# One encoder layer: the first modulation weights in two halves by columns, weights waited for by piece, turned logits copied in front of y

## The reference, cut to what matters

```python
mod = (silu(c) @ w_ada + b_ada).reshape(B, 6, D)   # shift1, scale1, gate1, shift2, scale2, gate2
h = rmsnorm(x, g_pre_mix) * (1 + scale1) + shift1
x = x + gate1 * rmsnorm(token_mixer(h), g_post_mix)    # h @ w_in, mLSTM heads | attention heads, @ w_out
h = rmsnorm(x, g_pre_ffn) * (1 + scale2) + shift2
aff = softmax(h @ w_router)                            # 16 experts, each takes its top 128 tokens
x = x + gate2 * rmsnorm(experts(h, aff), g_post_ffn)
```

## Time and profile before

| | |
|---|---|
| median of 3 runs | 2425.46 us (2424.74 to 2425.91) |
| profiled execution | 2422.2 us, span 2420.4 us |
| TensorE busy | 2286.9 us, 94% |
| DVE, ScalarE, GpSimd busy | 1206.9 us (50%), 1103.8 us (46%), 605.3 us (25%) |
| mean granted TensorE clock | 0.98 |
| start until the first product of h @ w_in | 37.8 us, TensorE busy 14.28 us of it |
| GpSimd, root of the mean squares (L792) | 1.05 us for the first quarter, 1.93 us for the second |
| GpSimd, split of half unit 1 of w_in (L803) | 2.54 us for two pieces, from 41.70 |
| DVE, normalising a quarter (L1371) | 2.74 us for four |

### The profile page before, as it was taken

How to read it: one execution, slowest core, us unless ns; L and a number is a source line. 1 busy time by engine, 2 the same in 40 slices (tenths; PEclk the granted TensorE clock), 3 DMA queues, 4 the chain that set the end, 5 groups by cost and what they waited for, 6 DMA issues and landing times. The chain is left out here.

```text
span 2420.4 us, 34918 instructions
## 1 busy us (share of the span) xinstructions
PE 2286.9 (94%) x13449; PEld 1905.4 (79%) x13449; DVE 1206.9 (50%) x1879; ACT 1103.8 (46%) x1826; POOL 605.3 (25%) x675
## 2 busy tenths in 40 slices
PE   6999999999999998999936999999999999999996
PEld 3679989777999896677725888888888888888885
DVE  3222334654323446665565555544445556666664
ACT  4223444655434436665532444444444454545552
POOL 3004332433143424430021011111010122222433
PEclk9999999999999999999967999999999999999998
DMA  8845445657464558764455566666666678888775
GB/s 311 250 119 185 144 159 190 196 149 178 115 201 136 191 163 233 217 184 155 170 212 220 195 224 210 224 215 216 204 204 232 212 277 305 321 313 291 278 290 165
DMA packets 239038, 511.46 MB, mean 211 GB/s; under 512 B 36981, under 2 KB 128005, under 8 KB 235825
## 3 DMA queue, kind: packets, MB, share of 16 engines
q1 hardware_dynamic: 190960, 394.78, 48.5%
q0 software_dynamic: 47936, 114.77, 16.1%
HBM read 415.32 MB, written 93.69 MB: 210 GB/s over the span
## 5 line engine op out<-in xcount | busy, mean ns | idle before, releaser
L2465 DVE TENSOR_TENSOR moe_w_lo<-moe_wf,moe_w_hi 128x2048 fp32r<-128x2048 f32 x192 | 439.6, 2292 | 457.0 <-ACT moe_w_hi L2343 457.0
L2343 ACT ACTIVATE moe_w_hi<-moe_wf 128x2048 fp32r<-128x2048 f32 x192 | 368.0, 1917 | 549.4 <-PE moe_acc L2575 549.3
L2575 PE MATMUL moe_acc<-moe_w_hi,moe_x_hi 128*128 128x512 f32 x1024 | 403.0, 394 | 1.7 <-DVE moe_x_lo L2471 1.4
L2575 PE MATMUL moe_acc<-moe_w_hi,moe_x_lo 128*128 128x512 f32 x1024 | 399.9, 391 | 0.0
L2575 PE MATMUL moe_acc<-moe_w_lo,moe_x_hi 128*128 128x512 f32 x1024 | 399.6, 390 | 0.0
L2575 PEld LDWEIGHTS moe_acc<-moe_w_hi,moe_x_hi 128*128 128x128 f32 x1024 | 193.0, 188 | 41.9 <-DVE moe_x_lo L2471 1.8
L2575 PEld LDWEIGHTS moe_acc<-moe_w_hi,moe_x_lo 128*128 128x128 f32 x1024 | 192.9, 188 | 40.6
L2575 PEld LDWEIGHTS moe_acc<-moe_w_lo,moe_x_hi 128*128 128x128 f32 x1024 | 193.1, 189 | 39.1
L1785 PE MATMUL banks<-fr_w_hi,fr_h_hi 128*128 128x256 f32 x768 | 223.2, 291 | 0.0
L1785 PE MATMUL banks<-fr_w_lo,fr_h_hi 128*128 128x256 f32 x768 | 217.0, 283 | 0.0
L1785 PE MATMUL banks<-fr_w_hi,fr_h_lo 128*128 128x256 f32 x768 | 217.0, 283 | 0.0
(11 more groups left out here) (282 smaller groups left out, 4055.8 us busy)
## 6 DMA issues: line engine op xcount, KB each, us to landing
moe_wf<-in_w_expert_gate SPq DMA_DIRECT2D x64, 1024.0 KB, 4.9
moe_wf<-in_w_expert_up SPq DMA_DIRECT2D x64, 1024.0 KB, 5.0
moe_wf<-in_w_expert_down SPq DMA_DIRECT2D x64, 1024.0 KB, 7.1
fr_w_raw<-in_w_units SPq DMA_DIRECT2D x28, 1024.0 KB, 6.6
fr_bias<-in_na_bias SPq DMA_DIRECT2D x16, 1520.0 KB, 11.4
fr_a_w<-in_w_ada POOLq DMA_DIRECT2D x16, 1024.0 KB, 8.8
scratch_qk_t<-fr_stage SPq DMA_DIRECT2D x64, 256.0 KB, 2.6
scratch_vov<-fr_stage SPq DMA_DIRECT2D x96, 128.0 KB, 2.2
```

What stands on the lines that cost most here:

```text
L2343: nc.scalar.activation(w_hi[:, q, :, :], wf[:, q, :, :], ACT.Copy).then_inc(w_hi_ready, 1)
L2465: nc.vector.tensor_tensor(w_lo[:, q, :, :], wf[:, q, :, :], w_hi[:, q, :, :].bitcast(F32), ALU.subtract).then_inc(w_lo_ready, 1)
L2575: mm = nc.tensor.matmul(acc[:, j, b, :], x[:, g, k, :], w[:, q, a, h * HALF:(h + 1) * HALF], start=(k == 0 and i == 0), stop=(k == KC - 1 ...
```

## The change

Three things. First, the first round of w_ada comes in sixteen pieces of 0.5 MB: for each k the columns 0 to 511 and 1024 to 1535 (the first half of shift1 and of scale1, rows of 2 KB), then half unit 0 of w_in, then the other columns. The first half of the modulation is multiplied, copied, turned and added alone, and k 0 to 3 of h and of blocks 0 and 1 are done on it; the second half's products stand between these four ticks, and the last two turns of x too. Second, a block waits for the first piece of its weights only, and for the second in the tick that uses it. Third, in the output stage `take_parts` stands in front of `take_y`. Some semaphores are shared to make room.

```diff
@@ SP
-                sp.dma_start(a_w[:, k, :], ada_view[k, :, 0:4 * HALF]).then_inc(a_first[k // 2], 16)
+                sp.dma_start(ada_part(a_w[:, k, :], 0), ada_part(ada_view[k, :, 0:4 * HALF], 0)).then_inc(a_first[k // 2], 16)
             load_w(0)
+            for k in range(KC):
+                sp.dma_start(ada_part(a_w[:, k, :], 1), ada_part(ada_view[k, :, 0:4 * HALF], 1)).then_inc(a_o_loaded[k], 16)
             load_x(1)
             load_w(1)
@@ ScalarE, output stage
+                    if 2 <= t <= N_TILES + 1 and t != N_TILES:
+                        take_parts(t - 2)
                     if t < N_TILES:
                         take_y(t, 0)
                         need(act, omean_ready, 2 * t - 1)
                         out_squares(h2[:, t % 2, :], 0, (0,))
-                    if 2 <= t <= N_TILES + 1 and t != N_TILES:
-                        take_parts(t - 2)
@@ ScalarE, start
-            for k in range(KC):
-                take_x(k)
-            act.drain()
-            a_row_first()
-            split_w(0, 0)
-            for k in range(KC):
-                make_h(0, k)
-                if k == 1:
-                    split_w(0, 1)
-                if k >= 4:
-                    squares(1, k - 4)
+            a_row_first(0)
+            for half in range(2):
+                for k in range(4 * half, 4 * half + 4):
+                    take_x(k)
+                act.drain()
+                split_w(0, half)
+                if half:
+                    a_row_first(1)
+                for k in range(4 * half, 4 * half + 4):
+                    make_h(0, k)
+            for j in range(4):
+                squares(1, j)
@@ DVE
+            def modulation(half):
+                dve.wait_ge(mod_turned, 2 + half)
+                ks = slice(4 * half, 4 * half + 4)
+                for which in range(2):
+                    turned_mods = ps[:, MOD_BANKS[half][which], 0:4 * GROUPS].rearrange("p (k g) -> p k g", g=GROUPS)
+                    bias_ = b_cols[:, which * KC + 4 * half:which * KC + 4 * half + 4]
+                    nc.vector.tensor_tensor(mods[:, which, ks, :], turned_mods, bias_.unsqueeze(2).to_broadcast([P, 4, GROUPS]), ALU.add)
+                dve.drain()
+                for g in range(GROUPS):
+                    a = nc.vector.scalar_tensor_tensor(scale[:, g, ks], mods[:, 1, ks, g], 1.0, g_pre[:, ks], ALU.add, ALU.mult)
+                a.then_inc(scale_ready, 1)
...
+            for half in range(2):
+                a_row_first(half)
+                modulation(half)
+                if half == 0:
+                    split_w(0, 0)
+                for k in range(4 * half, 4 * half + 4):
+                    split_h(0, k)
+                if half == 0:
                     split_w(0, 1)
-            mean_of(1)
             for piece in range(2):
                 split_w(1, piece)
+            mean_of(1)
@@ TensorE
+            def ada_first(k, half):
+                if half:
+                    pe.wait_ge(a_o_loaded[k], 16)
+                else:
+                    pe.wait_ge(a_first[k // 2], 32)
+                for j in (half, 2 + half):
+                    mm = nc.tensor.matmul(ps[32 * j:32 * j + 2, (PO, PA)[half], :], c_silu[:, k, :], a_w[:, k, j * HALF:(j + 1) * HALF],
+                                          start=(k == 0), stop=(k == KC - 1))
+                mm.then_inc((a_early, a_done)[half], 1)
...
-                        pe.wait_ge(w_lo_ready, 2 * hu + 2)
+                        pe.wait_ge(w_lo_ready, 2 * hu + 1)
                     need(pe, evac_done, b - 1)
                     for u in range(TICKS):
+                        if hu != GATE_UNIT and u == (1 if form(b)[2] == "t" else 2):
+                            pe.wait_ge(w_lo_ready, 2 * hu + 2)
...
             for k in range(KC):
-                ada(0, k)
+                ada_first(k, 0)
                 if k == 1:
                     pe.wait_ge(cols_loaded, 48)
                     nc.tensor.transpose(ps[:, PS, 0:2 * KC], b_rows[:, :], ident[0:2 * KC, 0:2 * KC]).then_inc(mod_turned, 1)
-                if 2 <= k < 6:
-                    turn_x(0, 2 * k - 4)
-                    turn_x(0, 2 * k - 3)
...
+            for k in range(6):
+                turn_x(0, k)
+                if k == 1:
+                    turn_mods(0)
+            for k in range(4):
+                fill.tick(1)
+                if k in (1, 2):
+                    turn_x(0, 5 + k)
+                ada_first(2 * k, 1)
+                ada_first(2 * k + 1, 1)
+            turn_mods(1)
```

More of the change, by code:

```diff
@@ L426, in front @@
         PX = 7
+        PA, MOD_BANKS = 3, ((2, 4), (5, 4))
+        first_bank = lambda k: k % 2 if k < 4 else 6 + k % 2
         A_ROUNDS = 3
@@ L1039, in take_x, with a_row_first @@
                 act.wait_ge(turned, k + 1)
[L1040 to L1045, removed]
+                nc.scalar.activation(h_raw[:, k, 0:HALF], ps[:, first_bank(k), :], ACT.Copy).then_inc(xT_ready, 1)
+            def a_row_first(half):
+                act.wait_ge((a_early, a_done)[half], KC)
+                at_ = slice(32 * half, 32 * half + 2)
+                nc.scalar.activation(a_row[at_, 0, :], ps[at_, (PO, PA)[half], :], ACT.Copy).then_inc(a_row_ready, 1)
             def make_h(q, k):
@@ L1079, in split_o @@
                 c, a = i // 4, i % 4
[L1080 removed]
+                act.wait_ge(a_o_loaded[i], 32)
                 cut = (slice(None), slice(2 * a, 2 * a + 2), slice(c * HALF, (c + 1) * HALF))
@@ L1183, in stream @@
                         if t == N_TILES:
-                            act.wait_ge(x1_half, 1)
+                            act.wait_ge(row_half, 1)
                             out_squares(ox[:, (t - 1) % 2, :], 1, (0,))
@@ L1379, in split_h, with a_row_first @@
                 nc.vector.tensor_tensor(h_lo[:, k, cut], h_raw[:, k, cut], h_hi[:, k, cut].bitcast(F32), ALU.subtract).then_inc(h_ready, 1)
[L1381 to L1384, removed]
+            def a_row_first(half):
+                dve.wait_ge((a_early, a_done)[half], KC)
+                at_ = slice(64 + 32 * half, 66 + 32 * half)
+                nc.vector.tensor_copy(a_row[at_, 0, :], ps[at_, (PO, PA)[half], :]).then_inc(a_row_ready, 1)
+            def modulation(half):
[9 more added lines that the diff above has]
+                a.then_inc(scale_ready, 1)
             def ada_row(r):
@@ L1522, in stream @@
                             dve.wait_ge(ox_loaded[j], 16 * ((t - 1) // 2 + 1))
-                            nc.vector.tensor_tensor(ox[:, j, cut], ox[:, j, cut], h2[:, j, cut], ALU.add).then_inc(x1_ready if cut.stop == D else x1_half, 1)
+                            nc.vector.tensor_tensor(ox[:, j, cut], ox[:, j, cut], h2[:, j, cut], ALU.add).then_inc(x1_ready if cut.stop == D else row_half, 1)
                     yield
@@ L1550, in stream @@
                             dve.drain()
-                            nc.vector.tensor_tensor(h2[:, j, cut], h2[:, j, cut], rows[g][:, 2, cut], ALU.add).then_inc(h2_ready if cut.stop == D else h2_half, 1)
+                            nc.vector.tensor_tensor(h2[:, j, cut], h2[:, j, cut], rows[g][:, 2, cut], ALU.add).then_inc(h2_ready if cut.stop == D else row_half, 1)
                     if 2 <= t <= N_TILES + 1 and t != N_TILES:
@@ L1737, in turn_x @@
                 for j in range(4):
-                    mm = nc.tensor.transpose(ps[:, PH if q else k % 2, j * P:(j + 1) * P], x[:, j, k * P:(k + 1) * P], ident[:, :])
+                    mm = nc.tensor.transpose(ps[:, PH if q else first_bank(k), j * P:(j + 1) * P], x[:, j, k * P:(k + 1) * P], ident[:, :])
                 mm.then_inc(turned, 1)
@@ L1742, in ada @@
                 n = r * KC + k
[L1743 to L1747, removed]
+                pe.wait_ge(a_loaded[n % ARING], 16 * (n // ARING))
+                if k == 0:
                     pe.wait_ge(a_row_ready, 4 * r)
@@ L1752, in ada, with turn_mods @@
                 mm.then_inc(a_done, 1)
+            def ada_first(k, half):
[7 more added lines that the diff above has]
+                mm.then_inc((a_early, a_done)[half], 1)
+            def turn_mods(half):
+                pe.wait_ge(a_row_ready, 2 * half + 2)
+                for which in range(2):
+                    at_ = slice(64 * which + 32 * half, 64 * which + 32 * half + 2)
+                    for k in range(4):
+                        mm = nc.tensor.transpose(ps[:, MOD_BANKS[half][which], k * GROUPS:(k + 1) * GROUPS], a_row[at_, 0, k * P:(k + 1) * P], ident[at_, at_])
+                mm.then_inc(mod_turned, 1)
             def turn_rows(g):
@@ L1855, in turn_h2 @@
                 if t == N_TILES - 1 and not half:
-                    pe.wait_ge(h2_half, 1)
+                    pe.wait_ge(row_half, 2)
                 else:
```

26 lines of the change are left out of this document (7 added, 19 removed).

## The result

The changed kernel takes 2431.75 us (median; 2427.28 to 2434.64), the kernel before in the same session 2425.03 (2423.07 to 2427.43): ratio 1.0026, interval 1.0019 to 1.0034. It is 6.7 us slower. The forecast was 2422.5 with a range up to 2428. The profiled execution is the slowest of its kernel, 2434.64 us (span 2432.8). A second profile of the same code has span 2428.0, and a second one of the kernel before 2422.8 (2420.4 the first time): 5.2 us apart.

A forecast was written before the change was run, and what follows sets the result against it. TensorE, busy for 94% of the span, was taken as the bound. Start 1.0, weights by piece 1.7 and turned logits 0.3 sum to 3.0 us won: 2422.5 us from a median of 2425.46, range 2417.5 to 2428.

The forecast's parts named there:

- The failed step: Start: 4 of a row's 8 modulation matmuls take 0.95 us, in the last pair and in each of four rounds.
- The first product: Start: first product of h at 27.7 us, 10.1 us earlier than before.
- The rounds: Start: k 0 to 3 in turns with the second modulation half take 10.5 us, a_done at 38.2.
- The chain behind them: Start, after a_done: copy, turning, scale, make_h and split_h take 3.85 us, giving k 4 at 42.0.
- the mechanism of the clock: Start: idle gaps bring TensorE to half clock; in the kernel before this cost about 2.2 us.
- both gaps: Start: TensorE gaps at 21.3 to 27.7 and 38.2 to 42.0 us, costing 1.9 and 2.0 to 2.2 us.
- the case with both stretches: Start: half clock after each of two gaps; turn_x(1, 0) at 57.1 us, 0 won.
- The refill of x: Start: load_x(1) issued near 35 to 37 us; x ready 19.6 us after the turns, at 54.5 or 56.4.
- rival (c): Start: turns of x come too late, each us of delay past 37.4 costs one; 2428.3 us, chance 0.10.
- Weights by piece: w_lo waits: 0.67 us at 102.77 won whole, 1.0 of 1.93 at 471.82 kept; 1.7 us together.
- Turned logits: Output stage, first eight tiles: waits for lT go, waits for fr_sc replace them; 0.3 us won, bounds 0 and 4.6.
- slower: Whole kernel: measured slower by more than the 4.85 us a measurement can tell apart; chance 0.08.

The follow-up runs named there:

- e3: Changed kernel, each half of the modulation multiplied as four parts of 256 columns in four column groups instead of two of 512 in two: 2428.17 us, ratio 1.0016.
- e8: e1 with the modulation halves cut into four parts of 256 columns, one per column group: 2427.08 us, ratio 1.0016.
- e1: Changed kernel with only the new start; weights by piece and moved logits undone: 2429.85 us, ratio 1.0020.
- e6: e3 with turns 6 and 7 of x moved earlier and ScalarE's take_x(4) to take_x(7) between its make_h: 2429.86 us, ratio 1.0025.
- e7: Changed kernel, two column groups kept, with turn 6 of x ahead of the first products and turn 7 behind the first tick: 2428.37 us, ratio 1.0021.
- e9: Kernel before with 8 and 20 idle transposes around the turning of the modulation, results never read: 2423.49 us, ratio 0.9999.
- e2: Kernel before with only weights by piece and the moved logits, old start kept: 2423.80 us, ratio 0.9999.
- g2: e6 with idle transposes, never read, filling TensorE's waits in the start: 2426.04 us, ratio 1.0009.
- e5: Kernel before with each k pair's products issued as column groups 0 and 2 first, then 1 and 3: 2423.41 us, ratio 0.9994.

## Why the prediction was wrong

**The failed step** is the price of TensorE's own matmuls in the rounds: "The last pair of k has 4 of the 8 matmuls of the 30.83 row, 0.95 us", and the same 0.95 in "four times (6 products 1.40 + 4 matmuls 0.95)". I halved a row because half of its matmuls were left. They were the matmuls of two of four column groups that run side by side, and each group's work was as long as before: measured 1.89 us at full clock and 3.34 to 3.58 at half. Four rounds have 9.0 us of them (3.34 and three times 1.89) for 3.8 forecast: 5.2 us, 3.8 from the price at full clock and 1.45 from the half clock in the first round. e3 against after and e8 against e1 show it: 1.04 for 1.89 in every row at full clock, and `turn_x(1, 0)` 4.2 us earlier in e8. By the medians it is less, 2.6 of the 6.7 us and 2.1 of e1's 5.8. By the same error the sum has no term for TensorE's work growing: the matmuls were the same number, but in time they were double.

**The first product** was to come at 27.7 and came at 29.05. The transfers were right (last pair at 20.3 forecast, 20.19 in e3; the second halves are never waited for). The last pair took the wrong price here too (22.3 for 21.25), and w_hi came at 25.48 where I had 24.2. SP took 1.09 us and not 0.55 for each of the first eight pieces (8.71 for eight, 4.37 before), so w_in went out at 10.43 and not near 6; TensorE waited for none of it.

**The rounds** were to end at 38.2, or 40.1 with the slow clock, and ended at 46.3: 1.35 from the first product, 5.2 from the matmuls, and 1.4 from the first six products at half clock (2.83 for 1.40).

**The chain behind them** was right: 3.85 us forecast from a_done to k 4, 4.0 measured (46.3 to 50.34). So was the mechanism of the clock: both gaps brought it down, the first more often than not, as I had put it (it fell in after, its repeat, e1, e6, e7 and e8, and not in e3, with the same wait of 2.93 us). Its price in before was not right: 2.2 us by pace alone, of which e9 gave back 0.65 at the end of blocks 0 and 1 and 0.06 at `turn_x(1, 0)`, for VectorE stood behind.

**turn_x(1, 0)** was to come at 57.1 in the case with both stretches and came at 64.13: 7.0 later, of which 6.2 were there at a_done.

**The refill of x** went out at 41.10, against a bound of "wrong if after 39". By rival (c) that should have cost 3.7 us. It cost nothing visible, since the products were later still; e7, and e6 beside e8, confirm it.

**Weights by piece.** 0.67 at 102.77 was won whole, as said. At 471.82 the wait for the copy of p and the start of the turning came as worked out, but of the 1.0 us nothing stayed, because the clock fell again: the lower end that I had named. In the traces the part is 0.7 us and not 1.7, and the time of e2 (0.3 us below before) does not tell it from nothing.

**Turned logits.** Waits for lT replaced by waits for `fr_sc` of the same size, as said: nothing that a run here can show.

**The chances.** Rival (c) had the sign and 2428.3, with another mechanism; no rival asked whether TensorE's own work grows. That gave 0.08 to slower. A version with the four groups and a full clock (g2) still doesn't beat before.

**Left open.** e3 and e8 are 4.1 and 3.7 us over before by their medians, but at `turn_x(1, 0)` only 1.6 and 2.8 over before's first profile and 0.8 and 2.0 over its repeat; by span 5.4 and 4.2, or 3.0 and 1.8. Their traces show where more is lost: e3 is at half clock from 942.9 to 946.3 and from 1127.2 to 1130.6 us and falls back by 1.3 and 2.0 there, e8 from 1126.1 to 1129.5, by 1.8. Before has neither stretch in its two profiles, but e5 and e9, whose times are before's, have the first. One trace of each kernel doesn't show how often they come, so the rest of the loss stays unexplained.
